# A two-layer diffusion transformer on one core: first modulation weights in 1024-column pieces, constants in two loads

## The chip, the cores and the metric

The kernel runs on one core of a Trainium2 chip. The metric is the device time of one execution in microseconds (us). Before the change it is 2006.72 us, the median of 3 executions (2002.47 to 2007.99). The kernel has an instruction stream for each engine: TensorE (PE), VectorE (DVE), ScalarE (ACT), GpSimd (POOL), and SyncE (SP), which here only issues DMAs. Loads from device memory to SBUF that SP issues share one hardware queue.

## What is computed

256 latent tokens and 256 context tokens of width 1024 pass through two layers. The part that matters here is the start of a layer:

```python
mod = (silu(c) @ w_ada[l] + b_ada[l])          # w_ada: (2, 1024, 6144), float32
sh1, sc1, gt1, sh2, sc2, gt2 = split(mod, 6)   # 1024 columns each; the same with c_ctx for the context
h  = rms_norm(x, g_mix[l]) * (1 + sc1) + sh1
z  = h @ w_in[l]                               # then three token mixers, gates, w_out, residual
# then the second norm with sh2, sc2, a router, 16 experts (gate, up, down of 1024 x 1024), residual
```

In layer 0 nothing of `h @ w_in` can start before `sh1` and `sc1`, the first 2048 of the 6144 columns of `w_ada[0]`, have been multiplied: 8 MB of weights, as 1024 rows of 8 KB.

## The kernel before

A planner (`make_plan`) writes one list of steps per layer, and each engine's program walks that list and takes the steps that are its own. Engines meet at counting semaphores.

**Weights** come through a ring in SBUF. In layer 0 it holds four pieces of 1 MB (2048 float32 in each of 128 partitions). `P.load` gives a piece its place and notes which earlier pieces lie there; SP, before it issues the load, waits until these are used up (`wait_released`). For a modulation piece that is the end of the matmuls on it (`used_tile`, a count of `blk_ready`); for a piece of `w_in` it is the end of the splits of it.

**Modulation** (`ada(l, c)`) is computed in chunks of 512 columns; c = 0 and 1 are the halves of `sh1`, c = 2 and 3 those of `sc1`. A chunk has two pieces, each with 4 of the 8 row blocks (128 rows) and 512 columns: 512 runs of 2 KB. Below, ada0 to ada3 are the four chunks of layer 0 at its start. PE waits for both pieces, then runs 8 matmuls of 512 columns (two k steps for each of four column strips of the array, line 1517; in the trace each shows as two). DVE copies the result out (line 1200), PE transposes it in four parts (line 1530), and DVE adds it up and adds the bias (lines 1213 to 1234). Then PE takes the next chunk.

**Program order at the start.** SP issues nine loads of constants (`CONST`, 912 KB: identity, rope tables, rotation, masks, selectors; and small rows), the four pieces of ada0 and ada1, then `X` and the context half of `X` (1 MB each), then the two pieces of ada2 and the two of ada3, which lie where those of ada0 and ada1 lay, then the router weights and sinks, then pieces of `w_in` (two for each of ac, ax, ab; 1 KB runs), the first two where ada2's lay, the next two where ada3's lay.

PE does: transposes of the constants (`pre`), ada0, ada1, ada2, ada3, the transposes of the normalised tokens (`trmod`, line 1540), and then the blocks of `h @ w_in`. Each block is three products per k step (lines 1557 to 1559), because weights and activations are split into a high and a low part: ACT casts the high part of the weights (WH, line 1020), DVE subtracts to get the low part (WL, line 1196). ACT does the two splits of the first blocks ahead of its `trmod` work (FT, line 1036), and DVE ahead of its own (HH, HL, lines 1249 and 1250). So the first product needs the first piece of `w_in`, the modulation, and the transposed tokens.

The line of SP on which the start turns, and the release of a piece:

```python
halves = [P.load([(0, (4, 512), ("w_ada", l, 512 * c, 512, 4 * r, 4))]) for r in range(2)]
...
for ch in halves:
    ch.used_tile = mm.ready
```

Of the kernel before, what the change touches and what calls it, by code (L numbers as in the profile page):

```python
# [22 lines left out]
D = 1024  # L23
# [3 lines left out]
DEPTH = 2  # L27
# [231 lines left out]
def make_plan():  # L259
# [34 lines left out]
    def run(atoms):  # L294
        for a in atoms:
            emit(a)

    def ada(l, c):
        def go():
            halves = [P.load([(0, (4, 512), ("w_ada", l, 512 * c, 512, 4 * r, 4))]) for r in range(2)]  # L300
            v, half = c // 2, c % 2
            mm = P.tile(dve=True)
            for ch in halves:
                ch.used_tile = mm.ready
            s = P.add("ada", l=l, v=v, half=half, chunk=halves, tile=mm)

            def turn():
                if v == GT2V:
                    s.out = [P.tile(dve=True) for _ in range(2)]
                else:  # L310
                    s.out = [P.tile(dve=True)]
                    P.mods += 1
                P.add("ada2", l=l, v=v, half=half, out=s.out, tile=mm)
            P.deferred.append(turn)
        return go
# [269 lines left out]
def hybrid_dit_kernel(nc, A, out):  # L585
# [7 lines left out]
    with ctx:  # L593
# [219 lines left out]
        def place(at_, shape):  # L813
            return ring[:, at_:at_ + shape[0] * shape[1]].rearrange("p (k n) -> p k n", k=shape[0])
# [27 lines left out]

        @block.sync
        def _(sp):
            sp.dma_start(CONST[:], A["consts"]).then_inc(const_in, 16)
            r96 = A["b_ada"].rearrange("l (r p) -> (l r) p", p=128)
            sp.dma_start(ROWS[0:96, 0, :], r96).then_inc(const_in, 16)
            sp.dma_start(ROWS[96:112, 0, :], A["g_mix"].rearrange("l (r p) -> (l r) p", p=128)).then_inc(const_in, 16)
# [6 lines left out]
            for l in range(DEPTH + 1):  # L855
                for s in P.steps[l]:
                    if s.kind == "load":
# [4 lines left out]
                        if s.chunk is P.chunks[3]:  # L862
                            sp.dma_start(X[:, 0:2, :], A["x"].rearrange("o (t p) d -> p (o t) d", p=128)).then_inc(x_in, 16)
                            sp.dma_start(X[:, 2:4, :], A["ctx"].rearrange("o (t p) d -> p (o t) d", p=128)).then_inc(ctx_in, 16)
                        if s.chunk is P.chunks[7]:
                            for l_ in range(DEPTH):
                                sp.dma_start(WR[:, l_, :, :].rearrange("p (h k) e -> p h k e", k=4), A["w_router"][l_].rearrange("(h p k) e -> p h k e", p=128, k=4)).then_inc(late_const_in, 16)
                            sp.dma_start(SINK[:].rearrange("p l h -> p (l h)"),
                                         bcast_rows(A["sw_sink"].rearrange("l h -> (l h)"))).then_inc(late_const_in, 16)
# [30 lines left out]
        def _(pool):  # L900
# [3 lines left out]
            def mask(x):  # L904

                if x.bias == 1:
                    pool.wait_ge(const_in, 16 * NCONST)
                pool.wait_ge(bias_in[x.bias % 2], 32 * ((x.bias + 1) // 2 if x.bias % 2 else x.bias // 2))
                nc.gpsimd.tensor_tensor(BIAS[x.at][:], BIAS[x.at][:], NAM, ALU.add).then_inc(bias_ready, 1)

# [62 lines left out]
        def _(act):  # L973
# [8 lines left out]

            def norm(s):

                nc.scalar.activation(PRIME[:, 15 + norms[0]:16 + norms[0]], SLOTS[:, 0:1], ACT.Sqrt)
                if s.which == 1:
                    act.wait_ge(dve_evicted, s.x_updated)
                for tt in range(s.ntt):
                    if s.which != 1 and s.layer > 0:
                        act.wait_ge(x_added, X0 + SCB0[s.layer] - SPG[s.layer - 1] + 2 * (tt + 1))  # L990
                    elif s.which == 0 and tt % 2 == 0:
                        act.wait_ge((x_in, ctx_in)[tt // 2], 16)
                    c = 512 if s.which == 1 else 0
                    last = nc.scalar.activation(SQ[:, tt, c:D], X[:, tt, c:D], ACT.Square, accum_out=SS[:, tt:tt + 1])
                last.then_inc(sq_ready, 1)
                norms[0] += 1
                act.wait_ge(var_ready, norms[0])
                nc.scalar.activation(SD[:, 0:s.ntt], VV[:, 0:s.ntt], ACT.Sqrt).then_inc(std_ready, 1)
                if s.kind == "norm":
                    act.wait_ge(rs_ready, norms[0])  # L1000
                    for c in range(2):
                        for tt in range(s.ntt // 2, s.ntt):
                            last = nc.scalar.activation(*xn_half(tt, c, s.which), ACT.Copy, scale=RS[:, tt:tt + 1])
                        last.then_inc(xn_act, 1)
# [144 lines left out]
        def _(dve):  # L1149
# [33 lines left out]
            for l in range(DEPTH + 1):  # L1183
                for s in P.steps[l]:
# [123 lines left out]
                    elif kind == "finish":  # L1308
# [6 lines left out]
                        elif b.out in ("sk", "sq"):  # L1315

                            dve.wait_ge(blk_ready, b.rot_tile.ready)
                            r = BLK[b.rot_tile.bank]
                            nc.vector.tensor_tensor(r[:, SEQ:2 * SEQ], r[:, 0:SEQ], ROPE[:, 1, :], ALU.mult)
                            link(nc.vector.tensor_tensor(QT[:, 0:SEQ], QT[:, 0:SEQ], ROPE[:, 0, :], ALU.mult))  # L1320
                            nc.vector.tensor_tensor(QT[:, 0:SEQ], QT[:, 0:SEQ], r[:, SEQ:2 * SEQ], ALU.add).then_inc(dve_evicted, 1)
# [15 lines left out]
                    elif kind == "score":  # L1337
# [2 lines left out]
                        sc, p_ = SB_[u2], PB[u2]  # L1340
                        dve.wait_ge(s_ready, x.u + 1)
                        sink = SINK[:, l, 2 * x.p + x.hh:2 * x.p + x.hh + 1]
                        if x.br == "sw" and l == 0 and x.p == 0:
                            dve.wait_ge(late_const_in, 16 * (DEPTH + 1))
                        if x.qt < 2:
                            if x.u >= 2:
                                dve.wait_ge(turn_ready, x.u - 1)
# [137 lines left out]
        def _(pe):  # L1485
            mm = nc.tensor.matmul

            def open_tile(t):

                if t.before is not None:  # L1490
                    sem_, v = released(t.before)
                    pe.wait_ge(sem_, v)
                return BLK[t.bank]

            xn = 0
            for l in range(DEPTH):
                first_block = True
                for s in P.steps[l]:
# [10 lines left out]
                    elif kind == "ada":  # L1509

                        t = open_tile(s.tile)
                        for ch in s.chunk:
                            pe.wait_ge(w_in[ch.n], ch.arrived)
                        w = [place(ch.at, (4, 512)) for ch in s.chunk]
                        for kk in range(2):
                            for j in range(4):
                                last = mm(t[32 * j:32 * j + 32, :], CS[:, 2 * j + kk, :], w[j // 2][:, 2 * (j % 2) + kk, :], start=kk == 0, stop=kk == 1,  # L1517
                                          tile_position=(0, 32 * j))
                        last.then_inc(blk_ready, 1)
                    elif kind == "ada2":  # L1520
# [41 lines left out]
                    elif kind == "finish":  # L1562
                        b = s.blk
                        if b.out == "v" or b.out == "out":
                            pe.wait_ge(act_evicted, b.tile.act)
                            t, src = open_tile(b.out_tile), VT[b.i % 2] if b.out == "v" else YT[b.d % 2]
                            for tt in range(b.n // 128):
                                last = nc.tensor.transpose(t[:, 128 * tt:128 * tt + 128], src[:, 128 * tt:128 * tt + 128], IDENT)
                            last.then_inc(blk_ready, 1)
                        elif b.out in ("sk", "sq"):  # L1570
                            pe.wait_ge(act_evicted, b.tile.act)
                            t = open_tile(b.rot_tile)
                            mm(t[:, 0:SEQ], ROT, QT[:, 0:SEQ], start=True, stop=True).then_inc(blk_ready, 1)
                    elif kind == "score":
                        x = s.unit
# [33 lines left out]
                    elif kind == "route":  # L1609
# [4 lines left out]

                        if l == 0:
                            pe.wait_ge(wr_padded, 1)
                            pe.wait_ge(late_const_in, 16 * (DEPTH + 1))
                        for kk in range(2):
                            for j in range(4):
                                c0 = (l * KD + 2 * j + kk) * NE  # L1620
# [117 lines left out]
```

## Time and profile before

| | |
|---|---|
| median of 3 executions | 2006.72 us |
| the profiled execution, its time | 2008.78 us |
| its span, first to last instruction | 2007.0 us |
| mean granted TensorE clock | 0.946 of full |
| PE busy | 1670.2 us (83%) |
| DVE, ACT, POOL busy | 738.2, 489.9, 101.9 us |
| DMA over the span | 544.79 MB, mean 271 GB/s |
| ada0 starts on PE | 12.50 us |
| ada2 starts on PE | 28.47 us |
| first product of `h @ w_in` | 49.10 us |

How to read it: times in rows are us from the first instruction of the span. The time of an execution is 1.78 us more than its span. In a table of windows each engine's busy time stands with its number of instructions, then the granted clock of TensorE as a share of 2.4 GHz, the busy share of the 16 DMA engines, and what they moved. A share near 1 means that the DMA engines have no free time (the modelled share can read a little over 1).

### The profile page before, as it was taken

The page shows a single profiled execution, that of the slowest core. Times are in us where ns is not written, and L with a number is a line of the kernel's source. Part 1 is how long each engine was busy: PE and PEld are TensorE (multiplying, and loading weights), DVE is VectorE, ACT ScalarE, POOL GpSimd, SP SyncE. Part 2 cuts the span into 40 slices and gives each one's busy share as a digit, 9 for nine tenths or more (in the row PEclk, how much of TensorE's full clock was granted, in tenths as well). Part 3 has the DMA queues.
Part 4 walks back from the last instruction along what each step waited for, and adds up shares of the span by engine and source line. Part 5 has one row for each costly group of instructions (what it writes and reads, how often), then busy time and mean ns, then how long its engine had stood idle before and what let it go on. Part 6 is the DMA issues. An engine that isn't in the chain of part 4 may idle for free.

```text
span 2007.0 us, 25433 instructions
## 1 busy us (share of the span) xinstructions
PE 1670.2 (83%) x10056; PEld 978.1 (49%) x10056; DVE 738.2 (37%) x1597; ACT 489.9 (24%) x1051; POOL 101.9 (5%) x149
## 2 busy tenths in 40 slices
PE   4999999989995988888797799989796777676765
PEld 2887777656673322222232498876583222222221
DVE  3355666654425112121111556766553110110102
ACT  3225555541124100000000435544342000000000
POOL 1001210000001000000000102200000000000000
PEclk7999999999997999999999899989998999999998
DMA  9332331116765799999999643335665999999996
GB/s 352 104 94 71 94 93 43 56 50 211 267 225 210 298 427 428 428 428 429 429 428 428 216 140 108 121 127 190 230 245 206 427 427 429 428 428 429 428 428 254
DMA packets 149788, 544.79 MB, mean 271 GB/s; under 512 B 7450, under 2 KB 97744, under 8 KB 125132
## 3 DMA queue, kind: packets, MB, share of 16 engines
q1 hardware_dynamic: 147308, 537.54, 68.0%
q0 software_dynamic: 2400, 6.16, 1.1%
q8 instruction: 52, 0.85, 0.2%
q14 instruction: 28, 0.23, 0.0%
HBM read 540.70 MB, written 2.98 MB: 271 GB/s over the span
## 4 chain that ended last, share of the span: by engine, by line
PE 44%; DMA 31%; DVE 13%; ACT 7%; issue 4%; SPq 0%; POOL 0%; DVEq 0%; ACTq 0%; POOLq 0%
DMA ring<-in_w_exp_down 28%; PE bank L1680 14%; PE bank L1557 7%; PE bank L1559 7%; PE bank L1558 7%; DVE WL L1196 3%; PE bank L1517 2%; PE bank L1709 2%; DMA ring<-in_w_in 2%; ACT WH L1020 1%; PE bank L1648 1%; ACT PB L1093 1%; DMA ring<-in_w_ada 1%; DVE PB L1351 1%; DVE SM L1353 1%
## 5 line engine op out<-in xcount | busy, mean ns | idle before, releaser
L1680 PE MATMUL bank<-ring,XEB 128*32 128x256 f32 (+1 forms) x3072 | 470.6, 620 | 101.0 <-DMA ring<-in_w_exp_gate 50.6
L1680 PEld LDWEIGHTS bank<-ring,XEB 128*32 128x32 f32 (+1 forms) x3072 | 141.5, 130 | 423.6 <-issue 267.0
L1557 PE MATMUL bank<-HH,WH 128*128 128x512 f32 (+1 forms) x864 | 308.4, 357 | 4.9 <-DVE WL L1196 4.3
L1558 PE MATMUL bank<-HL,WH 128*128 128x512 f32 (+1 forms) x864 | 303.7, 351 | 0.0
L1559 PE MATMUL bank<-HH,WL 128*128 128x512 f32 (+1 forms) x864 | 302.8, 350 | 0.0
L1196 DVE TENSOR_TENSOR WL<-ring,WH 128x1024 fp32r<-128x1024 f32 (+1 forms) x172 | 185.0, 1077 | 176.9 <-ACT WH L1020 176.2
L1680 PE MATMUL bank<-ring,HIDT 128*32 128x256 f32 (+1 forms) x1536 | 187.7, 488 | 54.2 <-DMA ring<-in_w_exp_down 35.7
L1020 ACT CAST WH<-ring 128x1024 fp32r<-128x1024 f32 (+1 forms) x172 | 158.0, 924 | 136.8 <-DMA ring<-in_w_in 59.4
L1557 PEld LDWEIGHTS bank<-HH,WH 128*128 128x128 f32 x864 | 166.9, 193 | 42.1 <-issue 19.0
L1559 PEld LDWEIGHTS bank<-HH,WL 128*128 128x128 f32 x864 | 166.5, 193 | 21.6
L1558 PEld LDWEIGHTS bank<-HL,WH 128*128 128x128 f32 x864 | 166.8, 193 | 20.6
L1466 DVE TENSOR_TENSOR YE<-bank,GT 32x512 f32<-32x512 f32 (+1 forms) x128 | 70.8, 553 | 265.8 <-PE bank L1680 264.5
L1137 ACT ACTIVATE TH<-bank 128x512 f32<-128x512 f32 (+1 forms) x32 | 15.7, 490 | 564.8 <-PE bank L1680 564.8
L1680 PEld LDWEIGHTS bank<-ring,HIDT 128*32 128x32 f32 (+1 forms) x1536 | 67.9, 126 | 155.9 <-issue 67.3
L1456 DVE SCALAR_TENSOR_TENSOR TH<-TH,bank 128x512 f32<-128x512 f32 (+1 forms) x32 | 17.7, 554 | 253.9 <-ACT TH L1137 253.9
L1460 DVE TENSOR_TENSOR HID<-TH,bank 128x512 f32<-128x512 f32 (+1 forms) x32 | 17.7, 554 | 239.5 <-PE bank L1680 239.5
L1141 ACT ACTIVATE HIDT<-bank 128x512 f32<-128x512 f32 (+1 forms) x32 | 15.7, 490 | 297.9 <-PE bank L1693 297.9
L1517 PE MATMUL bank<-ring,CS 128*32 128x512 f32 x384 | 58.5, 736 | 23.2 <-ACT GT L1068 12.2
L1557 PE MATMUL bank<-OH,WH 128*128 128x512 f32 (+1 forms) x192 | 67.8, 353 | 8.9 <-DVE OL L1384 4.1
L1709 PE MATMUL bank<-YE,STB 128*128 128x512 f32 x96 | 55.3, 725 | 20.4 <-DVE YE L1466 20.4
L1593 PE MATMUL bank<-CONST,PB 128*128 128x128 f32 x320 | 53.8, 284 | 16.4 <-DVE PB L1378 16.4
L1092 ACT ACTIVATE PB<-PB,SM 128x256 f32<-128x256 f32 x64 | 32.6, 509 | 141.1 <-DVE SM L1354 141.1
(192 smaller groups left out, 1797.2 us busy)
## 6 DMA issues: line engine op xcount, KB each, us to landing
ring<-in_w_exp_gate SPq DMA_DIRECT2D x64, 2048.0 KB, 23.8
ring<-in_w_exp_up SPq DMA_DIRECT2D x64, 2048.0 KB, 25.4
ring<-in_w_exp_down SPq DMA_DIRECT2D x64, 2048.0 KB, 25.6
ring<-in_w_ada SPq DMA_DIRECT2D x48, 1024.0 KB, 7.4
ring<-in_w_in SPq DMA_DIRECT2D x40, 1024.0 KB, 5.6
ring<-in_w_in SPq DMA_DIRECT2D x28, 512.0 KB, 5.0
ring<-in_w_branch SPq DMA_DIRECT2D x24, 512.0 KB, 6.6
ring<-in_w_out SPq DMA_DIRECT2D x8, 1024.0 KB, 7.9
```

The source lines that it names most:

```text
L1020: nc.scalar.copy(WH[b.b % NWS][:, 0:b.kk, :], w).then_inc(split_hi, 1)
L1092: nc.scalar.activation(p_[:, 0:SEQ], p_[:, 0:SEQ], ACT.Exp, bias=NM[u2], accum_out=ES[u2][:, 0:1])
L1093: last = nc.scalar.activation(p_[:, SEQ:TOK], sc[:, SEQ:TOK], ACT.Exp, bias=NM[u2], accum_out=ES[u2][:, 1:2])
L1196: nc.vector.tensor_tensor(WL[b.b % NWS][:, 0:b.kk, :], w, WH[b.b % NWS][:, 0:b.kk, :].bitcast(f32), ALU.subtract).then_inc(split_lo, 1)
L1466: last = nc.vector.tensor_tensor(YE[32 * eo:32 * eo + 32, q, nw * c:nw * c + nw], YAB[rows, 0:nw], GT2[32 * eo:32 * eo + 32, q, nw * c:nw ...
L1517: last = mm(t[32 * j:32 * j + 32, :], CS[:, 2 * j + kk, :], w[j // 2][:, 2 * (j % 2) + kk, :], start=kk == 0, stop=kk == 1, tile_position= ...
L1557: mm(t, wh, hi[:, k, 0:b.n], start=k == 0, stop=False)
L1558: mm(t, wh, lo[:, k, 0:b.n], start=False, stop=False)
L1559: last = mm(t, wl, hi[:, k, 0:b.n], start=False, stop=k == b.kk - 1)
L1593: last = nc.tensor.transpose(TB[x.u % 2][:, 128 * c:128 * c + 128], PB[x.u % 2][:, 128 * c:128 * c + 128], IDENT)
L1680: last = mm(out_bank[tw * c:tw * c + tw, 0:nw], stationary[:, k, 0:tw], w[:, c::G] if spread else w[:, nw * c:nw * c + nw], start=k == 0, ...
L1709: mm(SCB[i % 2][:], STB[:, q, 128 * j:128 * j + 128], YE[:, q, 512 * h:512 * h + 512], start=True, stop=True).then_inc(sc_ready, 1)
```

## The change

The four chunks at the start of layer 0 are loaded otherwise: for `sh1` and for `sc1` there are four pieces, each with 2 of the 8 row blocks and all 1024 columns (256 runs of 4 KB), and both chunks of a pair read all four pieces. Number and size of the pieces, the place of each in the ring, and the matmuls are as before. A piece's `used_tile` is now that of the second chunk of its pair. Of `CONST` only the identity (64 KB, runs of 512 B) is loaded first; the rest (848 KB) is loaded behind the eighth piece, ahead of the router weights, and those that read it first wait for it. The sinks' wait in the scores on DVE goes; the wait at the first rope covers it. The activation that brings in ACT's square-root table reads the identity instead of the slot numbers.

```diff
     def ada(l, c):
         def go():
-            halves = [P.load([(0, (4, 512), ("w_ada", l, 512 * c, 512, 4 * r, 4))]) for r in range(2)]
             v, half = c // 2, c % 2
+            if l == 0 and v == SH1 or l == 0 and v == SC1:
+                if half == 0:
+                    wide[:] = [P.load([(0, (2, D), ("w_ada", l, D * v, D, 2 * r, 2))]) for r in range(4)]
+                pieces = list(wide)
+            else:
+                pieces = [P.load([(0, (4, 512), ("w_ada", l, 512 * c, 512, 4 * r, 4))]) for r in range(2)]
             mm = P.tile(dve=True)
-            for ch in halves:
+            for ch in pieces:
                 ch.used_tile = mm.ready
-            s = P.add("ada", l=l, v=v, half=half, chunk=halves, tile=mm)
+            s = P.add("ada", l=l, v=v, half=half, chunk=pieces, tile=mm)
...
-            sp.dma_start(CONST[:], A["consts"]).then_inc(const_in, 16)
+            sp.dma_start(IDENT, A["consts"][:, 0:128]).then_inc(const_in, 16)
...
                         if s.chunk is P.chunks[7]:
+                            sp.dma_start(CONST[:, 128:], A["consts"][:, 128:]).then_inc(late_const_in, 16)
                             for l_ in range(DEPTH):
...
                 if x.bias == 1:
-                    pool.wait_ge(const_in, 16 * NCONST)
+                    pool.wait_ge(late_const_in, 16 * (DEPTH + 2))
...
-                nc.scalar.activation(PRIME[:, 15 + norms[0]:16 + norms[0]], SLOTS[:, 0:1], ACT.Sqrt)
+                nc.scalar.activation(PRIME[:, 15 + norms[0]:16 + norms[0]], IDENT[:, 0:1], ACT.Sqrt)
...
+                            if b.rope == 1:
+                                dve.wait_ge(late_const_in, 16 * (DEPTH + 2))
...
-                        if x.br == "sw" and l == 0 and x.p == 0:
-                            dve.wait_ge(late_const_in, 16 * (DEPTH + 1))
...
-                        w = [place(ch.at, (4, 512)) for ch in s.chunk]
+                        if len(s.chunk) == 4:
+                            w = [place(ch.at, (2, D))[:, kk, 512 * s.half:512 * s.half + 512] for ch in s.chunk for kk in range(2)]
+                        else:
+                            w = [place(ch.at, (4, 512))[:, kk, :] for ch in s.chunk for kk in range(4)]
...
+                            if b.rope == 1:
+                                pe.wait_ge(late_const_in, 16 * (DEPTH + 2))
...
-                            pe.wait_ge(late_const_in, 16 * (DEPTH + 1))
+                            pe.wait_ge(late_const_in, 16 * (DEPTH + 2))
```

SP's program at the start, before the change, from the last load of constants (`ROWS<-in_conv_w`) to the first pieces of `w_in` (a row with xN stands for N like it, each with the wait shown):

```order
L854 DMA ROWS<-in_conv_w 24x128
L861 DMA ring<-in_w_ada 128x4x512 x4
L863 DMA X<-in_x 128x2x1024
L864 DMA X<-in_ctx 128x2x1024
L861 DMA ring<-in_w_ada 128x4x512 [waits blk_ready] x4
L867 DMA WRP<-in_w_router 128x2x64 x2
L868 DMA SINK<-in_sw_sink 128x16
L861 DMA ring<-in_w_in 128x8x256 [waits blk_ready] x4
```

And the same place with the change:

```order
L861 DMA ROWS<-in_conv_w 24x128
L868 DMA ring<-in_w_ada 128x2x1024 x4
L870 DMA X<-in_x 128x2x1024
L871 DMA X<-in_ctx 128x2x1024
L868 DMA ring<-in_w_ada 128x2x1024 [waits blk_ready] x4
L873 DMA CONST<-consts 128x1696
L875 DMA WRP<-in_w_router 128x2x64 x2
L876 DMA SINK<-in_sw_sink 128x16
L868 DMA ring<-in_w_in 128x8x256 [waits blk_ready] x4
```

The order of the loads is the same but for `CONST`. What the rows don't show is the count that each wait asks for. Before, the fifth and sixth piece wait for ada0, the seventh and eighth for ada1; the first two of `w_in` wait for ada2, the next two for ada3. Now the fifth to eighth all wait for ada1, and all four of `w_in` for ada3.

PE's program at the same place, before, from ada0 to the first matmul of ada2 (`w_in0` to `w_in7` are the landing counts of the pieces in turn):

```order
L1517 MATMUL bank<-ring,CS 32x512 [waits w_in1,w_in0,cs_ready]
L1517 MATMUL bank<-ring,CS 32x512 x7
L1530 MATMUL bank<-CONST,MB 128x128 [waits dve_evicted]
L1530 MATMUL bank<-CONST,MB 128x128 x3
L1517 MATMUL bank<-ring,CS 32x512 [waits w_in3,w_in2,act_evicted]
L1517 MATMUL bank<-ring,CS 32x512 x7
L1530 MATMUL bank<-CONST,MB 128x128 [waits dve_evicted]
L1530 MATMUL bank<-CONST,MB 128x128 x3
L1517 MATMUL bank<-ring,CS 32x512 [waits w_in5,w_in4,dve_evicted]
```

With the change:

```order
L1528 MATMUL bank<-ring,CS 32x512 [waits w_in2,w_in1,w_in3,w_in0,cs_ready]
L1528 MATMUL bank<-ring,CS 32x512 x7
L1541 MATMUL bank<-CONST,MB 128x128 [waits dve_evicted]
L1541 MATMUL bank<-CONST,MB 128x128 x3
L1528 MATMUL bank<-ring,CS 32x512 [waits w_in2,w_in1,w_in3,w_in0,act_evicted]
L1528 MATMUL bank<-ring,CS 32x512 x7
L1541 MATMUL bank<-CONST,MB 128x128 [waits dve_evicted]
L1541 MATMUL bank<-CONST,MB 128x128 x3
L1528 MATMUL bank<-ring,CS 32x512 [waits w_in6,w_in5,w_in7,w_in4,dve_evicted]
```

No matmul moved. ada0 now waits for four pieces instead of two, and so does ada2; ada1 and ada3 wait for nothing that the chunk ahead of them had not.

## Rows read from the trace of the kernel before

**Rows 1.** Windows by stage: engines' busy time (count), PEclk, DMA share, GB/s.

```profile
53.70:300.00 246.30, 242.16 (x1155) 195.21 (x1155) 133.66 (x288) 103.03 (x213) 34.17 (x48) 0.99 0.29 87
...
480.00:590.00 110.00, 107.17 (x549) 75.08 (x547) 46.07 (x77) 23.50 (x38) 0.00 (x0) 1.00 0.74 254
...
659.00:1050.00 391.00, 333.17 (x1422) 109.69 (x1424) 71.48 (x105) 16.72 (x28) 11.80 (x20) 0.98 0.99 419
...
1560.00:2007.00 447.00, 316.57 (x2910) 104.36 (x2902) 52.32 (x114) 15.48 (x37) 6.06 (x16) 0.93 0.96 409
```

**Rows 2.** Chain that ended last, first 50 us: start, duration, what.

```profile
4.64 7.73 DMA ring<-in_w_ada
...
12.50 3.67 PE bank L1517 x16
...
16.60 11.73 DMA ring<-in_w_ada
...
28.47 3.68 PE bank L1517 x16
...
32.17 0.70 DVE MB L1200
...
32.92 1.12 PE bank L1530 x4
34.03 3.14 PE bank L1517 x16
...
39.44 2.27 DVE WL L1196 x2
...
49.16 0.74 PE bank L1557
```

**Rows 3.** Timeline, 16 to 50 us: start, duration, instruction, [idle before, releaser].

```profile
16.95 0.66 PE L1530 MATMUL bank<-CONST,MB 128*128 128x128 f32 x4 [0.80 <-DVE MB L1200]
...
17.91 1.92 PE L1517 MATMUL bank<-ring,CS 128*32 128x512 f32 x16 [0.31 <-DMA ring<-in_w_ada]
...
20.37 1.06 ACT L994 ACTIVATE SQ<-X 128x1024 f32<-128x1024 f32 x1 [9.19 <-DMA X<-in_x]
...
22.93 1.06 ACT L994 ACTIVATE SQ<-X 128x1024 f32<-128x1024 f32 x1 [0.37 <-DMA X<-in_ctx]
...
32.16 27.99 SPq L861 DMA_DIRECT2D ring<-in_w_in  x6
...
37.48 1.99 ACT L1020 CAST WH<-ring 128x1024 fp32r<-128x1024 f32 x2 [8.26 <-DMA ring<-in_w_in]
...
39.54 1.93 ACT L1036 ACTIVATE FT<-bank,MOD 128x256 f32<-128x256 f32 x4
```

**Rows 4.** Line 861 in 4:12, 60:75 and 420:440 us: loads, issue to landing.

```profile
L861 SPq DMA_DIRECT2D ring<-in_w_ada x4: 405/504/938, 4.2 to 5.7; - x4
...
DMA to landing us min/median/max: 5.5/8.8/12.0
...
L861 SPq DMA_DIRECT2D ring<-in_w_in x2: 367/367/367, 59.8 to 70.7; - x2
...
DMA to landing us min/median/max: 5.3/5.3/5.4
...
L861 SPq DMA_DIRECT2D ring<-in_w_ada x2: 367/368/368, 423.2 to 431.6; - x2
...
DMA to landing us min/median/max: 4.9/4.9/4.9
```

**Rows 5.** Windows: PE busy time (count), PEclk, DMA share, GB/s.

```profile
4.00:5.00 1.00, 0.00 (x0) 1.00 0.84 311
5.00:6.00 1.00, 0.00 (x0) 1.00 0.82 138
...
22.50:32.10 9.60, 3.63 (x16) 0.52 1.05 387
49.10:53.30 4.20, 4.20 (x11) 0.50 0.93 380
```

More of the change, by code:

```diff
@@ L296, in run @@
             emit(a)
+    wide = []
     def ada(l, c):
         def go():
-            halves = [P.load([(0, (4, 512), ("w_ada", l, 512 * c, 512, 4 * r, 4))]) for r in range(2)]
             v, half = c // 2, c % 2
+            if l == 0 and v == SH1 or l == 0 and v == SC1:
[4 more added lines that the diff above has]
+                pieces = [P.load([(0, (4, 512), ("w_ada", l, 512 * c, 512, 4 * r, 4))]) for r in range(2)]
             mm = P.tile(dve=True)
-            for ch in halves:
+            for ch in pieces:
                 ch.used_tile = mm.ready
-            s = P.add("ada", l=l, v=v, half=half, chunk=halves, tile=mm)
+            s = P.add("ada", l=l, v=v, half=half, chunk=pieces, tile=mm)
             def turn():
@@ L1513, in _ @@
                             pe.wait_ge(w_in[ch.n], ch.arrived)
-                        w = [place(ch.at, (4, 512)) for ch in s.chunk]
+                        if len(s.chunk) == 4:
+                            w = [place(ch.at, (2, D))[:, kk, 512 * s.half:512 * s.half + 512] for ch in s.chunk for kk in range(2)]
+                        else:
+                            w = [place(ch.at, (4, 512))[:, kk, :] for ch in s.chunk for kk in range(4)]
                         for kk in range(2):
                             for j in range(4):
-                                last = mm(t[32 * j:32 * j + 32, :], CS[:, 2 * j + kk, :], w[j // 2][:, 2 * (j % 2) + kk, :], start=kk == 0, stop=kk == 1,
+                                last = mm(t[32 * j:32 * j + 32, :], CS[:, 2 * j + kk, :], w[2 * j + kk], start=kk == 0, stop=kk == 1,
                                           tile_position=(0, 32 * j))
```

## The prediction

> **What bounds the kernel now.** I read the windows of the whole run first, to see what a shift of the start is worth later. After the start, PE computes 242.16 of 246.30 us up to 300 us, and most of what follows up to 590 us [rows 1]. The two expert stages run with the DMA engines 96 to 99% busy, but their loads cannot run ahead of the dense part: SP issues the first ones behind waits for PE's tiles at the end of it. So a delay of the first product of `h @ w_in` moves everything behind it by as much, and nothing later makes up for it. All else is a question of the first 50 us.
>
> There I read the chain of waits. It goes through SP issuing the first piece, its transfer, ada0, then SP issuing the fifth piece, its transfer, ada2, ada3, the low part of the first `w_in` weights on DVE, and the first product at 49.1 us [rows 2]. Then the timeline around it, for what ends each wait: ada1 waits only 0.31 us for its pieces (17.91), `X` lands at 20.4 and the context at 22.9, ada2 waits for the DMA, and ACT sits idle 8.26 us before the first cast of `w_in` weights at 37.48 [rows 3]. The windows show why: between 22.5 and 32.1 us the DMA engines are at 1.05 and 387 GB/s [rows 5]. The start is bound by the DMA stream, and this stream is kept full by an interlock: when ada0 has ended at 16.2 us, SP can issue pieces five and six behind `X`, long before `X` has landed. The reader is to see that releasing ring pieces early is what keeps the DMA busy, and that PE works in the shadow of it.
>
> **The first four pieces.** They are issued from 4.2 to 5.7 us, because nine loads of constants stand ahead on SP, each with its issue time. The change keeps all of them, so the first piece is still issued at about 4.2. It landed 5.5 us later (9.7), the fourth 12.0 us after 5.7 (17.7) [rows 4], thus 2.7 us apart. Two things make them faster. (a) 848 KB of `CONST` are gone ahead of them. That would be 2.2 us at 387 GB/s, but the slice 5 to 6 us moved only 138 GB/s [rows 5]: the constants were nearly through, and the weights had not begun to flow. A piece on an empty queue takes 4.9 us in runs of 2 KB [rows 4]. So the first can land at about 9.0 in place of 9.7; the gain is 0.7, between 0 (landing as now) and 0.9. (b) Runs of 4 KB. `X` and the context, 1 MB each in such runs, landed at 20.37 and 22.93, 2.56 us apart [rows 3], against 2.7: 0.15 to 0.2 us for each piece. With 2.55 us a piece the fourth lands at 9.0 + 3 x 2.55 = 16.65, and ada0, which now needs all four, starts at about 16.8 in place of 12.50. That is 4.3 later.
>
> The Trainium skill ("DMA: Bandwidth & Descriptors", Specifications) has line rate from runs of 512 B on, so by it the longer runs would bring nothing. Rows 3 and 4 speak against it, by a small amount, and the sum with it instead would be about 1.1 us later: 0.6 at the fourth piece, 0.5 at the eighth (estimate, from the spacings in those rows).
>
> **ada0 and ada1.** Between them nothing changes: 3.67 us of matmuls, the copy, and ada0's transposes up to 17.61, that is 5.1 us from ada0's start at 12.50 [rows 2, 3]. ada1 then needs 1.92 us and no wait. It ends at 16.8 + 5.1 + 1.92 = 23.8 us.
>
> **The stream runs dry.** SP now holds pieces five to eight until the end of ada1, 23.8 us; pieces five and six went at 16.2 before. The queue ahead of them holds only `X` and the context, which land 2.5 and 5.1 us after the fourth piece, at 19.2 and 21.8. So the DMA engines stand still from about 21 until the new transfers flow. The fifth piece pays the price of an empty queue again, 4.9 less 0.2: landed at 28.5. Three more follow at 2.55: 36.15. ada2 needs all four and starts at 36.3 in place of 28.47, 7.8 later. (`X` lands a little earlier than now, so the norm behind it, which was not on the chain, stays off it.)
>
> **ada2, ada3 and the first w_in.** ada2 takes 3.68 us, the copy 0.70, the transposes 1.12, ada3 3.14; with the gaps it is 8.7 us from ada2's start to ada3's end, 37.17 now [rows 2]. All of it ran at the lower clock, the granted share being 0.52 after PE had stood waiting [rows 5]. PE waits even longer now, so I keep these times. ada3 ends at 45.0. Before, the first piece of `w_in` was issued at 32.16, when ada2 had ended, and landed in time for the cast at 37.48, 5.3 us later [rows 3]; in the shadow of that ran ada3. Now its place is that of the fifth piece, free only after ada3: issued at 45.0. The late constants, 0.9 MB, are through at about 39, so the queue is empty; a piece of `w_in` then takes 5.3 us [rows 4]. The cast is at 50.3 in place of 37.48, 12.8 later.
>
> One thing is given back. DVE was ready for the first low part only at 39.44 [rows 2], held by the end of ada3's sums, though the first cast had ended at 38.5 (1.99 us for two [rows 3]). Now ada3's sums are long done, and DVE begins a cast, 1.0, after 50.3: 51.35 in place of 39.44. That is 11.9 later. The rest up to 49.1, the FT and HH chain with GpSimd's copy beside it, hangs on these two and keeps its length; three further pieces of `w_in` are issued together at 45, and land by about 58.5, before their blocks are due.
>
> **The rest of the edits at nothing.** The constants behind the eighth piece land near 39 us. Their readers come after the first product in program order: first the mask on GpSimd, then the ropes, then the router. If they were late, the mask would hold the first attention score, which has the blocks of ac, ax, ab and the values ahead of it on PE. Reading the identity for the square root, and the sinks' wait moved to the rope, cost no instruction more. SP issues one DMA more, 0.4 us, ahead of the `w_in` loads but in the time in which it waits for ada3.
>
> **The sum.** First four pieces and two of them more to wait for, +4.3; released by ada1 rather than ada0, on an empty queue, with all four needed, +3.5 more (7.8 at ada2); `w_in` behind ada3, +5.0 more; DVE's slack, -0.9. Together +11.9. Against the profiled execution of 2008.78 us this gives 2020.7. That execution lies 2.06 above the median of the three, so I forecast for a median 2006.72 + 11.9 = 2018.6 us, 0.6% more. About 0.3%, 6 us, is what a measurement of this kernel can tell from no change.
>
> **Bounds.** First piece without gain, +0.7; runs of 4 KB without gain, +1.1; ada1 at the lower clock, as ada0 had it (3.67 for 1.92), +1.75. In the other direction: a piece behind an idle queue at its lowest price, 2.55 for its own bytes and nothing fixed, would take 2.2 off at the fifth piece and 2.6 at the first of `w_in`; neither is likely to be whole. ada2 and ada3 both at the full clock would take 3.0 off. For the mechanism alone I take +8 to +14, and with the scatter of the medians 2013 to 2021.
>
> **The rivals.**
>
> *The stream stays full (not slower beyond the measurement).* Bytes ahead of the first product are the same or fewer: `CONST` off is 2.2 us, eight pieces 0.15 to 0.2 shorter each 1.4, together 3.6 us earlier for the eighth piece. For this ada1 would have to end before the context has landed, at 21.8, less the 2 us that a transfer needs to start. Then the eighth piece, whose bytes were through near 34 before, would land near 30.4, ada2 would start 2 later than now, and with +5.0 and -0.9 for the `w_in` pieces the end would be some 6 later, 2012.8, the edge of no change; with ada2 and ada3 at the full clock 3.0 less, 2009.8. For it speaks that the DMA engines were the bound, against it that ada1 would need to end 4 us ahead of the 23.8 above. It decides below about 20 us. 10%.
>
> *Something later takes up the delay.* If the first expert loads or the expert stage were bound by a stream that did not wait for the start, the 11.9 would shrink. Its point is whether the expert loads' issue moves with the dense part. The waits named above say that it does; 3% for a time within 6 us of before, near 2010, and 2% for a gain by chance of the clock.
>
> *The longer runs bring nothing.* The pieces stay 2.7 apart and the first lands at 9.7. Then the fourth is there at 17.8 and ada0 starts 1.1 later than in my sum, and the fifth to eighth add 0.7: 13.7 in all, 2020.4. The row for `X` against that for the weights speaks against it; for it, that two landings are all the evidence. 10%. This is where the page's rule named above leads.
>
> *PE's clock costs more.* ada1 at the lower clock, as ada0 had it, is 1.75 more: 2020.4. The full pace of ada1 at 17.91 [rows 3] speaks against it, and that its neighbours keep their distance; for it, that ada2 and ada3 ran slowly after a pause. 10%.
>
> The likeliest case as worked out, 65%. Slower by over 0.3%: 0.65 + 0.10 + 0.10, and none of the others, 0.85; within 0.3%: 0.12; faster: 0.03. The range takes in both dearer cases, the bounds above, and half of the full stream's case: 2012.5 to 2021.5.
>
> **What would show it.** In the profile after: ada0 on PE at 16 to 18 us (at 14 or below, step one is wrong); ada1 with no DMA wait; SP's fifth to eighth issue in one go at 23 to 25 us; a window near 22 to 25 us with the DMA share far below 1; ada2 at 35 to 38 us; all four `w_in` issues after ada3; ACT idle for over 10 us ahead of its first cast near 50; the first product at 59 to 63 us. From there to the end each stage as long as before. The forecast falls if the DMA share stays near 1 through 20 to 30 us, if a stage behind 60 us is shorter, or if ada2 and ada3 run at the full clock.

## The result, and the profile after

The changed kernel took 2016.95 us (median of 6 executions, 2014.55 to 2020.2) against 2003.71 for the kernel before (6 executions, 2001.79 to 2007.99). The ratio is 1.006, with a 95% interval of 1.0046 to 1.0073: slower by 9 to 15 us. The forecast was 11.9 more, 0.6%, and 2018.6 us, counted from the median of 2006.72 us of the three executions known before; over all six that median is 3.0 lower. From 2003.71 the forecast would read 2015.6.

The profiled execution after took 2014.55 us and its span is 2012.7, at a mean granted clock of 0.949. First its chain of waits over the first 66 us (start, duration, what), which answers to [rows 2]:

```profile
5.65 11.52 DMA ring<-in_w_ada
...
17.30 3.56 PE bank L1528 x16
...
20.89 0.70 DVE MB L1208
...
21.63 0.66 PE bank L1541 x4
22.29 1.90 PE bank L1528 x16
...
25.64 11.85 DMA ring<-in_w_ada
...
37.63 3.64 PE bank L1528 x16
...
42.04 0.66 PE bank L1541 x4
42.70 1.90 PE bank L1528 x16
44.61 5.32 DMA ring<-in_w_in
...
49.95 1.05 ACT WH L1028
...
51.03 2.36 DVE WL L1204 x2
...
60.83 0.74 PE bank L1568
```

The reader should see three long transfers where there were two. ada0 starts at 17.30 (12.50 before), ada2 at 37.63 (28.47), and there is a link that the chain before did not have: from ada3's end at 44.6 to the landing of the first `w_in` piece. The timeline has the first product:

```profile
60.78 0.80 PE L1568 MATMUL bank<-HH,WH 128*128 128x512 f32 x1
```

It was at 49.10. So 11.68 us are lost in the start. The windows of the profile after (PE busy, PEclk, DMA share, GB/s) show where the DMA engines stood:

```profile
4.00:5.00 1.00, 0.00 (x0) 1.00 0.07 19
...
21.00:22.00 1.00, 0.37 (x3) 1.00 0.39 156
22.00:23.00 1.00, 1.00 (x11) 1.00 0.00 0
23.00:24.00 1.00, 1.00 (x12) 1.00 0.00 0
24.00:25.00 1.00, 0.18 (x5) 1.00 0.00 0
25.00:26.00 1.00, 0.61 (x4) 1.00 0.73 90
...
28.00:33.00 5.00, 0.00 (x0) 0.50 1.02 415
```

Before, no second from 7 to 32 us was below a share of 1. Now nothing moves from about 21.7 to 25, and there is a second gap: nothing moves from 41 to 45 while SP waits for ada3.

What follows keeps its length at first. The weight loads at the line of the attention scores, with their first and last start, before and after:

```profile
L1585 PEld LDWEIGHTS bank<-stk,dup x96: 186/190/337, 160.2 to 1314.1; 128*128 128x128 f32 x96
```

```profile
L1598 PEld LDWEIGHTS bank<-stk,dup x96: 186/190/333, 171.7 to 1324.4; 128*128 128x128 f32 x96
```

The first scores are 11.5 later. The windows by stage, moved by 11.7 us, show the dense part unchanged and the second expert stage up to the end 441 us long for 447 in [rows 1]:

```profile
65.40:311.70 246.30, 242.16 (x1156) 195.13 (x1154) 134.35 (x288) 102.99 (x213) 33.22 (x48) 0.99 0.30 87
...
1571.70:2012.70 441.00, 311.54 (x2878) 104.49 (x2870) 52.35 (x114) 15.18 (x37) 6.06 (x16) 0.93 0.97 411
```

So the two spans differ by only 5.7 us, and the medians by 13.2. The profiled execution after was the fastest of its six, and the one before (2008.78 us) was slower than all of its six. The start of the gather of the tokens for the experts in the second layer, before and after, shows how much of the delay is left there:

```profile
L1648 PE MATMUL bank<-SELT,XNH x16: 389/389/795, 1524.4 to 1533.1; 128*128 128x512 f32 x16
```

```profile
L1661 PE MATMUL bank<-SELT,XNH x16: 387/392/795, 1532.4 to 1541.0; 128*128 128x512 f32 x16
```

It is 8.0 us of the 11.5, and 5.7 at the end. The missing part comes and goes between executions of one kernel. The stretch from the last weight loads of the scores in layer 0 to its first gather (443.1 to 639.3 before) took 196.2 us before and 193.5 with the change, but 191.4 in a second profile of the changed kernel. The stretch from the second layer's gather to the end took 482.6 before and 480.3 with the change, but 482.5 and 480.5 in two profiles of another kernel (the one with the first `w_in` piece at its own place). So two profiles cannot show whether a later stage takes something up; the medians can, and they differ by 13.2 us (12 by the ratio), no less than the start does.

I compare the kernels below by the start of their first product, which differed by 0.7 and 0.1 us in the two kernels profiled twice, and by medians where timed.

### The profile page after: what moved, and what is told of

Its sections match the earlier page's. It is cut to its first block, busy times and chain, and to the rows that moved or that the text cites. A ratio compares the mean times of both kernels' runs of the same rounds, so it can differ in the third digit from the quotient of the medians.

```text
span 2012.7 us, 25439 instructions
## 1 busy us (share of the span) xinstructions
PE 1661.9 (83%) x10056; PEld 978.7 (49%) x10056; DVE 739.3 (37%) x1597; ACT 489.3 (24%) x1051; POOL 101.1 (5%) x149
## 4 chain that ended last, share of the span: by engine, by line
PE 43%; DMA 32%; DVE 13%; ACT 7%; issue 5%; SPq 0%; POOL 0%; DVEq 0%; ACTq 0%; POOLq 0%
DMA ring<-in_w_exp_down 28%; PE bank L1693 13%; PE bank L1568 7%; PE bank L1569 7%; PE bank L1570 7%; DVE WL L1204 3%; DMA ring<-in_w_in 2%; PE bank L1722 2%; PE bank L1528 2%; ACT WH L1028 2%; PE bank L1661 1%; DMA ring<-in_w_ada 1%; ACT PB L1101 1%; DVE PB L1359 1%; DVE SM L1361 1%
## 5 line engine op out<-in xcount | busy, mean ns | idle before, releaser
L1528 PE MATMUL bank<-ring,CS 128*32 128x512 f32 x384 | 51.3, 656 | 33.7 <-DMA ring<-in_w_ada 22.5
```

## The experiments

There were eleven runs: nine other kernels, one of them twice, and the changed kernel once more. "First product" is the start of the first matmul of `h @ w_in` in the profile: 49.10 us before, 60.78 after.

### The constants alone

```diff
-            if l == 0 and v == SH1 or l == 0 and v == SC1:
+            if False:
```

> The split of the constants alone, pieces of the modulation weights as before the change. What is compared is the start of the first product of h @ w_in in the profile (49.10 us before, 60.78 us after). Theory A (the wide pieces and what they hold back make the whole loss): 49 to 51, since the late constants, 848 KB or about 2.2 us of transfer, now stand ahead of the first w_in piece in a full queue, of which the first pieces give back at most 0.7. Rival B (a good part of the loss is the constants' new place): 53 or more. Rival C (the constants were worth their time at the front): 47 or less.

First product 50.35 us, one execution of 2005.29. As theory A has it. Its chain:

```profile
4.63 7.72 DMA ring<-in_w_ada
...
12.49 3.68 PE bank L1528 x16
...
28.47 3.67 PE bank L1528 x16
...
32.16 7.36 DMA ring<-in_w_in
...
39.55 1.05 ACT WH L1028
```

ada0 starts at 12.49, the same as with 848 KB more ahead: with narrow pieces the constants at the front cost nothing. The first piece is issued at 4.2 in both, behind the same nine issues on SP, and lands 5.5 us later in both. Behind the eighth piece they stand in a full queue ahead of `w_in`, which lands 2.1 us later (cast at 39.55 for 37.48). DVE's slack takes up 0.8 of it.

### The wide pieces alone

> The wide pieces alone, all constants first as before the change. Theory A: first product at 60.5 to 62 us, as with the whole change or up to 1 later, and about 2013 to 2018 us, ratio 1.005 to 1.007. Rival B: 57 or less, ratio under 1.004.

```diff
-            halves = [P.load([(0, (4, 512), ("w_ada", l, 512 * c, 512, 4 * r, 4))]) for r in range(2)]
...
+                    wide[:] = [P.load([(0, (2, D), ("w_ada", l, D * v, D, 2 * r, 2))]) for r in range(4)]
...
             sp.dma_start(CONST[:], A["consts"]).then_inc(const_in, 16)
```

It is the change without its lines on `CONST` and the waits for it. First product 63.35, median 2019.23 (4 executions), ratio 1.0072 (1.0054 to 1.009). The direction is theory A's, but the ratio is just above its range (1.005 to 1.007), and the first product is 1.35 later than its bound. The chain has most of the cause:

```profile
17.77 3.68 PE bank L1527 x16
...
22.21 1.12 PE bank L1540 x4
23.33 3.47 PE bank L1527 x16
```

The transposes took 1.12 us and ada1 3.47, where the changed kernel's profile has 0.66 and 1.90. That is the price of the case "PE's clock costs more" in the prediction, in this one profile, and it holds the fifth piece until 26.8. That it is the clock is not shown: the granted clock reads 1.00 from 17 to 28 us here, though 3.47 us is close to what the same matmuls take where it reads 0.50. A second, smaller part: ada0 starts at 17.77, 0.5 later than with the change, so with wide pieces the constants at the front do cost something. The first piece landed 5.8 us after its issue, for 5.3.

### Narrow pieces, released late

```diff
             for ch in halves:
                 ch.used_tile = mm.ready
+            if l == 0 and c in (0, 2):
+                wide[:] = halves
+            if l == 0 and c in (1, 3):
+                for ch in wide:
+                    ch.used_tile = mm.ready
```

> Narrow pieces as before the change, constants as before, but the ring places are given back as late as with wide pieces: those of ada0 at the end of ada1, those of ada2 at the end of ada3. Theory A (release by the second chunk does it): the fifth piece is issued at 19.8 us, near the context's landing at 22.9, so ada2 is little later, 28.5 to 30; the first w_in piece is issued at 37 to 38.5 and cast at 42.5 to 44; first product at 53 to 55.5 us. That would leave 6 to 8 us of the loss to the need for four pieces at once. Rival D (late release is all of it, four pieces at once cost nothing of their own): 60 or more. Rival E (release costs nothing, only four pieces at once do): 49 to 50.

First product 54.50, one execution of 2011.39: 5.4 lost by the release alone, theory A. As the expectation says, that leaves 6.3 of the 11.7 to what the rest of the change adds on top of a late release, the need for four pieces at once above all. SP issues the fifth piece at 21.34 and the first of `w_in` at 38.38, and ACT waits:

```profile
21.34 2.47 SPq L868 DMA_DIRECT2D ring<-in_w_ada  x4
...
43.66 1.99 ACT L1027 CAST WH<-ring 128x1024 fp32r<-128x1024 f32 x2 [14.51 <-DMA ring<-in_w_in]
```

ada1 took 3.29 us for 1.92 before (with the granted clock reading 1.00 in both), which is why the fifth piece was issued at 21.34 and not at the expected 19.8. Even so ada2 started at 29.49, only 1.0 later than before. With narrow pieces `X` and the context still cover most of the late release; it is the `w_in` piece behind ada3 that costs.

### Wide pieces with their own places

On top of the change, pieces five to eight go to the last two ring slots, which are used for other data only later.

```diff
-                    wide[:] = [P.load([(0, (2, D), ("w_ada", l, D * v, D, 2 * r, 2))]) for r in range(4)]
+                    wide[:] = [P.load([(0, (2, D), ("w_ada", l, D * v, D, 2 * r, 2))], at=4 * SLOT + 2 * D * r if v == SC1 else None) for r in range(4)]
```

`load` takes the place from `at` where it is given, and leaves alone the position at which the next piece of the ring goes.

> The change, but pieces five to eight (wide) have places of their own in SBUF, in the last two ring slots that nothing uses so early, so that SP waits for nothing and the DMA queue stays full. Theory A (the stand-still of the DMA behind the late release makes the loss): no window with the DMA share under 0.9 between 7 and 35 us; ada2 at 31.5 to 34; the w_in pieces are issued after ada1, about 24; ada3 ends 7 to 8.7 us after ada2's start; first product at 49 to 53 us; ratio to before within 0.998 to 1.003. Rival (four pieces at once make the loss whatever the queue does): first product at 56 or more, ratio over 1.003.

First product 51.44, median 2009.28 (10 executions), ratio 1.0021 (1.0011 to 1.0032). Theory A. The stream is full and ada2 starts 4.8 us ahead of the changed kernel's; `w_in` pieces wait only for ada1:

```profile
14.21 18.50 DMA ring<-in_w_ada
...
32.85 3.35 PE bank L1531 x16
...
41.79 2.27 DVE WL L1207 x2
```

```profile
21.00:22.00 1.00, 0.22 (x1) 1.00 1.03 414
22.00:23.00 1.00, 1.00 (x8) 1.00 1.04 418
23.00:24.00 1.00, 1.00 (x8) 1.00 1.03 410
24.00:25.00 1.00, 1.00 (x8) 1.00 0.99 397
```

(The first fence is of the chain, the second of the windows.) ada3 ended 6.7 us after ada2's start, a little less than the 7 to 8.7 expected, and its sums and not the `w_in` piece hold the first product: the cast of the weights runs at 38.53, DVE's low part waits until 41.79. Of the 11.7 us, 9.3 are gone with the two waits on SP. No matmul, no piece and no byte differs from the changed kernel.

### The first w_in piece with its own place, twice

```diff
-            return [P.load([(0, (8, 256), ("w_in", l, COL[name] + 256 * r, 256))]) for r in range(2)]
+            return [P.load([(0, (8, 256), ("w_in", l, COL[name] + 256 * r, 256))], at=4 * SLOT if l == 0 and name == "ac" and r == 0 else None) for r in range(2)]
```

> The change, but the first w_in piece has a place of its own in SBUF (the region of the values, written later), so that it is issued behind the sinks without a wait for ada3. All else as with the change. Theory A (the w_in piece behind ada3 is worth 5.0 less 0.9 us): ada2 at 37.6 to 38.5 as with the change, the cast of w_in weights before 44, and the first product at 55 to 57.5 us. Rival (the norm and transposes behind ada3 would have set the same time anyway): 60 to 61.

First product 58.03, one execution of 2014.11. Off the range of theory A by 0.5. The cast runs at 44.0 and no longer sets the time; instead the chain goes through ada3, which took 3.06 us here against 1.90. The granted clock stayed at 0.50 until about 45.3. To see whether that was chance, the same kernel ran again with timing:

> The kernel with the first w_in piece at a place of its own once more. Its first profile had the first product at 58.03, 2.75 ahead of the change, with ada3 and its transposes at the lower clock (3.06 and 1.12 us against 1.90 and 0.66). Theory H: at like clock the first product is at 56.3 to 56.7 and at the lower one near 58.0, so the piece behind ada3 is worth 4.1 to 4.4. Rival: 58 with ada3 at 1.9, so the worth is 2.75. Ratio to before 1.003 to 1.006.

First product 57.97, median 2010.27 (10 executions), ratio 1.0034 (1.0019 to 1.005). Theory H's case of the lower clock, near 58.0. The chain has it again:

```profile
37.32 3.68 PE bank L1531 x16
...
41.77 1.12 PE bank L1544 x4
42.88 3.18 PE bank L1531 x16
```

The piece behind ada3 was worth 2.1 to 2.8 us as run. With ada3 and its transposes at the 1.90 and 0.66 us of the changed kernel the first product would be at 56.2 to 56.4, which is 3.9 to 4.4 less (an estimate from these rows, near the 4.1 of my sum); neither profile of this kernel showed it. The lower clock fills part of what the wait leaves.

### The late constants later still

```diff
-                        if s.chunk is P.chunks[7]:
+                        if s.chunk is P.chunks[11]:
                             sp.dma_start(CONST[:, 128:], A["consts"][:, 128:]).then_inc(late_const_in, 16)
+                        if s.chunk is P.chunks[7]:
```

> The change, with the late constants issued behind the twelfth piece (the last w_in piece at the start) instead of behind the eighth. In the profile after the change the eighth piece landed at 37.49 us, 13.3 after the fifth's issue, where I had counted 12.35. Theory F (bytes of the late constants and router weights, issued 2 us behind, take turns with the last weights' bytes): eighth piece lands at 36.4 to 36.9. Rival G (the DMA engines end a piece at different times, and the last counts, whatever stands behind): 37.3 to 37.6.

One execution of 2016.26, first product 60.31. ada2 started at 37.13, so the eighth piece landed at 37.0, between the two theories' ranges. From the fifth's issue it took 12.9 us, against 13.3 in the first profile of the change. But it took 12.9 too in both profiles of the kernel above and in the second profile of the changed kernel, where the constants were issued at 26.4 to 26.9, as in the first (26.5). So the constants' bytes are not what I had missed, and 0.4 us of the 13.3 is scatter. Line by line, issue to landing of the four pieces, changed kernel at 24 to 27 us and this one:

```profile
L868 SPq DMA_DIRECT2D ring<-in_w_ada x4: 368/468/811, 24.2 to 25.6; - x4
...
DMA to landing us min/median/max: 5.6/8.8/11.8
```

```profile
L868 SPq DMA_DIRECT2D ring<-in_w_ada x4: 368/468/979, 24.1 to 25.5; - x4
DMA to landing us min/median/max: 5.2/8.3/11.5
```

The first piece on an empty queue with three behind it lands 5.2 to 5.6 us after its issue, the rest 2.55 apart. The narrow pieces released late took 5.3.

### Narrow pieces with their own places

```diff
-                pieces = [P.load([(0, (4, 512), ("w_ada", l, 512 * c, 512, 4 * r, 4))]) for r in range(2)]
+                pieces = [P.load([(0, (4, 512), ("w_ada", l, 512 * c, 512, 4 * r, 4))], at=4 * SLOT + 2048 * (2 * (c - 2) + r) if l == 0 and c in (2, 3) else None) for r in range(2)]
...
-                        if s.chunk is P.chunks[7]:
+                        if s.chunk is P.chunks[9]:
                             sp.dma_start(CONST[:, 128:], A["consts"][:, 128:]).then_inc(late_const_in, 16)
```

The starting point is the kernel with the constants alone (`if False:`).

> Narrow pieces as before the change, five to eight at places of their own (no wait on SP), the rest of the constants behind the tenth piece, so ahead of nothing that the first product needs. The stream is full from 6 us on and carries 11.7 MB to the first w_in piece. Theory A: ada2 at 27.5 to 28.5, ada3 at 32 to 34, the first cast of w_in weights before 38, first product at 46.5 to 48.5 us, 1 to 2.5 less than before, which is below what the timing tells: ratio 0.998 to 1.000. Rival: the context's norm and ACT's order keep 49.

First product 48.20, median 2004.75 (12 executions), ratio 0.9999 (0.999 to 1.0008). As expected: 0.9 better at the start, nothing that the timing tells. The landing of the first `w_in` piece sets the time:

```profile
37.39 1.99 ACT L1032 CAST WH<-ring 128x1024 fp32r<-128x1024 f32 x2 [8.26 <-DMA ring<-in_w_in]
```

Against the wide pieces at their own places it is 3.2 us better (51.44 less 48.20) with the queue full in both. That is not the price of the width by itself, since the late constants stand elsewhere too: behind the first two `w_in` pieces here, ahead of them there. The kernel with the constants alone has them ahead of the `w_in` pieces as well, and against it the wide pieces at their own places lose only 1.1 (51.44 less 50.35).

### Weights ahead of the constants, two pieces and one

SP issues two pieces of weights before the nine loads of constants, on top of the kernel above; then the same with one piece.

```diff
+                        if s.chunk is P.chunks[1]:    # P.chunks[0] in the second kernel
+                            constants()
```

> As the one before, and SP issues the first two pieces of modulation weights ahead of all constants. The slice 4 to 6 us, nearly empty with the change, should fill: the weights begin to flow near 2.3 us. Theory A: ada0 at 9.5 to 11, ada2 at 25 to 27, first product at 44 to 46.5 us, 3 to 5 less than before, ratio 0.997 to 0.999. Rival: the small constants behind 2 MB of weights land so late that ada0 waits for them and starts at 12 or later; then 47 to 49.

First product 47.08, median 2003.67 (12 executions), ratio 0.9993 (0.9983 to 1.0004). The rival was right: the constants landed at 10.8 and ada0 waited for DVE's work on them, until 13.29:

```profile
10.84 0.45 PE L1519 MATMUL bank<-CONST,ROWS 112*128 112x112 f32 x1 [10.84 <-DMA ROWS<-in_conv_w]
...
13.29 3.64 PE L1536 MATMUL bank<-ring,CS 128*32 128x512 f32 x16 [1.17 <-DVE CS L1206]
```

> As the kernel with two pieces issued ahead of the constants, but with one. There the constants landed at 10.8 and held ada0 until 13.29. With 1 MB less ahead of them they should land near 8.2 to 8.8, the modulation's input be ready near 11, and ada0 start at 10.8 to 11.8; ada2 at 25.5 to 27, the first product at 46 to 47.5 us, 1.6 to 3 less than before, ratio 0.998 to 1.000. Rival: the stream and not ada0 sets what follows, so nothing is gained on the kernel with two: 46.9 to 47.3.

First product 46.28, median 2003.33 (12 executions), ratio 0.9989 (0.998 to 0.9998): the earliest first product here, 2.8 us ahead of the kernel before. The constants landed at 8.12 and ada0 started at 10.58, a little ahead of the range; ada2 at 26.48. The gain of 0.1% only just clears its interval, and is below the 0.3% that I had named as what a measurement of this kernel can tell. The 0.8 us between the two kernels are not all the constants': with two pieces ada3 ran at the lower clock (3.50 us) and was on the chain, with one it took 1.92 and the chain went through the landing of the `w_in` piece.

### The changed kernel again

The same code, so there is no edit.

> The changed kernel once more, for a second profile. In its first profile ada2, the copy, the transposes and ada3 took 6.98 us where 8.70 were taken from before; ada3 ran at the full clock (1.90 for 3.14). Theory H (when the clock comes back varies from one execution to the next, so this 1.7 is no property of the change): in a new profile ada3 may take anything from 1.9 to 3.7, and the first product starts at 60.3 to 62.8, its lateness against 60.78 being that of ada3 and the transposes. Rival (fixed by the change): ada3 1.9 again, first product within 0.3 of 60.78. Ratio to before 1.005 to 1.0075.

Median 2019.02 (4 executions), ratio 1.0077 (1.0057 to 1.0097; 1.005 to 1.0075 was expected), first product 60.08. ada3 took 1.90 again:

```profile
42.18 1.90 PE bank L1528 x16
```

So theory H has nothing for it from this kernel. The rival's 1.90 held, its 0.3 us did not: the fourth piece landed 0.1 earlier, the eighth another 0.4 (ada2 at 37.08), and the `w_in` piece took 5.14 for 5.32.

## Why the prediction was right, step by step

**The first four pieces.** Forecast: ada0 at 16.8; measured 17.30. The spacing of 2.55 us held. The first piece landed at 9.5, not 9.0. The constants' removal gave 0.2 where the sum had 0.7; with narrow pieces it gave nothing (same ada0 as before), with wide pieces 0.5 (17.77 without it).

**The runs of 4 KB.** The Trainium skill's line rate from 512 B ("DMA: Bandwidth & Descriptors", Specifications) does not describe these rows: a full window moved 387 GB/s with runs of 2 KB [rows 5] and 415 with runs of 4 KB (28 to 33 us after). For a piece of 1 MB that is 0.15 to 0.2 us (2.55 apart for 2.7), a gain that exists and is far too small for what it costs.

**ada0 to ada1's end.** 7.0 forecast, 6.9 measured. But 9.0 in the profile with the wide pieces alone, so the clock rival's price is a real part of the scatter; its 1.75 left out the transposes, which were 0.46 longer. The prediction says that ada0 ran at the lower clock. The record doesn't show it: before, the granted clock reads 1.00 through ada0 (12 to 17 us), whose matmuls took 3.67 us, and falls to 0.50 only at 23. Why these matmuls take twice as long in ada0 as in ada1 stays open.

**The stream runs dry.** As forecast in place and kind: SP issues four pieces at 24.20, with the DMA engines idle before. The size was off: ada2 started at 37.63 in place of 36.3. Of these 1.3 us 0.4 were handed down from ada0's start; the rest is the step that failed, the price of "an empty queue again, 4.9 less 0.2": it was 5.6, and 5.2 in the second profile.

**ada2 to ada3's end.** The second step that failed: "I keep these times". 8.7 forecast, 6.97 measured, and the same in three profiles of kernels with that schedule. PE had stood longer, and the granted clock was 0.50 from 28 us as I had expected, but it came back at 41.0, as ada2 ended:

```profile
40.00:41.00 1.00, 1.00 (x8) 0.50 0.00 0
41.10:42.00 0.90, 0.12 (x4) 1.00 0.00 0
```

Before it had come back only at 36.5, late in ada3.

**w_in behind ada3.** 5.3 forecast, 5.32 measured; cast at 49.95 (50.3), low part at 51.03 (51.35), first product at 60.78 (61.0). The two misses cancelled, +1.3 and -1.7, and that is luck: the start came out within 0.3 us of the sum, while two of its stretches were off by more than 1 us each.

**Nothing later takes it up.** Shown by the profiles only up to about 450 us (11.5 later there too), and by the timed kernels as a row: first product later by 14.3, 11.7 and 2.3 us than before, ratio 1.0072, 1.006 and 1.0021, which on 2005 us are 14, 12 and 4 us. The kernel with the first `w_in` piece apart fits less well (8.9 later, 6.8 slower, interval 3.8 to 10), and the changed kernel's second timing lies at 15 (11.4 to 19.5) for 11.0.

**The rival of the full stream** was not one for this kernel, but it is what the kernel with own places does: there the loss shrinks to 2.3 us, and not to the 6 that I gave it, since the `w_in` pieces were then free of ada3 too. Its other term was too small: with the stream full the eighth piece landed at 32.7, not 30.4, so ada2 was 4.4 later than before and not 2.

**The signs.** The prediction named three things by which it would fall. The DMA share did not stay near 1. ada3 did run at the full clock, ada2 did not up to its end. And a stage behind 60 us was shorter, the window of the second expert stage by 6 us against the profile before. Of these only 2.3 lie behind the gather of that layer (482.6 and 480.3 us to the end), the rest ahead of it, and both are of the size of the scatter between profiles of one kernel; the medians keep the whole delay. So this sign was too sharp for single profiles. That ada3 ran at the full clock belongs to the term that failed: it is the -1.7 above.

The whole loss, by kernels in a row, each step from single profiles: the late constants ahead of the `w_in` pieces, 1.25 us (49.10 to 50.35); the width with a full queue, 1.1 (to 51.44, where pieces five to eight also have places of their own); the two waits on SP that the shared release brings, 9.3 (to 60.78). That is 11.7. The parts depend on each other. The late release alone costs 5.4 with narrow pieces and 9.3 with wide ones: with narrow ones ada1 ended at 21.3, when the queue still had bytes to move, with wide ones at 24.2, when it had none since 21.7. Nor is it shown that the two waits on SP divide as the sum says, 3.5 and 4.1: one was run alone and gave 2.1 to 2.8, for the clock's reason above.

What stays open is when the granted clock returns. ada3 ran at the full clock in the three profiles of the changed schedule and at the lower one in both of the kernel with the `w_in` piece apart, whose ada2 started at 37.49 and 37.32, inside the 37.08 to 37.63 of those three. Nothing here tells why.

## What to carry to other kernels

A ring piece is worth as much for what its release lets start as for how it loads. Whoever makes a piece larger in the dimension in which its users come one after the other delays the release of all of them to the last user. Price that first, by asking whether the queue still has work until then; the gain of longer runs, here 0.15 to 0.2 us for a piece of 1 MB, comes after.

A load moved "behind" in a full queue stands ahead of something else. Moved from a spot where the queue was short of issued loads, the constants saved 0 to 0.5 us there and held the `w_in` piece up by 2.1 us at the new place, of which 1.25 reached the first product.

## What was not expected of the hardware

A 1 MB piece at the head of four on an empty queue lands 5.2 to 5.6 us after its issue, with runs of 2 KB as of 4 KB. A lone piece in the kernel before took 4.9 [rows 4], but in the profile after such lone pieces took 5.2. The following ones come 2.55 us apart with runs of 4 KB, so about half of the 5.2 to 5.6 is not transfer (an estimate from these two numbers).

The granted clock fell to half after the pause behind ada1 and came back at different points of the same sequence, 1.9 or 3.1 to 3.5 us for the same 8 matmuls, in kernels that differ only in the place and time of one `w_in` load.
